# Joint attentions: sample keys in two halves a unit, two tiles turned per step, softmax in place, values and outputs for two heads

## The chip, the cores and the metric

The kernel runs on one core of one Trainium2 chip. The time is device microseconds (us) of one execution, median of several runs. The profiled execution is a further one, so its sums are made against its own time. TensorE (PE) multiplies, VectorE (DVE) and ScalarE (ACT) work element by element, GpSimd (POOL) prepares constants, and SyncE (SP) issues every transfer of the stages spoken of here, one after the other.

## The reference, cut to what matters

One inference step of a two-layer encoder: layer 0 has window attention (A) and differential attention (B), layer 1 a forgetting attention (C). Each mixer is applied to a prompt of 1024 frames and to eight running streams of 16 new frames each, whose keys and values of the past (2048 frames) lie in caches. A SwiGLU layer follows each mixer. What is computed in the part that changes:

```python
def _diff_attend(q, k, v, qpos, kpos, lam):        # B: 4 heads, 2 score maps each
    q2 = q.reshape(b, tq, B_HEADS, 2, HEAD_DIM)
    k2 = k.reshape(b, tk, B_HEADS, 2, HEAD_DIM)
    scores = jnp.einsum('bthed,bshed->bhets', q2, k2).astype(jnp.float32) * SCALE
    p = jax.nn.softmax(jnp.where(mask, scores, NEG_INF), axis=-1)
    attn = p[:, :, 0] - lam * p[:, :, 1]
    return jnp.einsum('bhts,bshd->bthd', attn.astype(v.dtype), v)

def _fox_attend(q, k, v, cq, ck, qpos, kpos):      # C: 16 heads
    scores = jnp.einsum('bthd,bshd->bhts', q, k).astype(jnp.float32) * SCALE
    scores = scores + jnp.moveaxis(cq, 1, 2)[..., :, None] - jnp.moveaxis(ck, 1, 2)[..., None, :]
    p = jax.nn.softmax(jnp.where(kpos[None, :] <= qpos[:, None], scores, NEG_INF), axis=-1)
    return jnp.einsum('bhts,bshd->bthd', p.astype(v.dtype), v)
```

All arrays are float32. HEAD_DIM is 64.

## The kernel before, in words

The program runs stages one after the other, each with its own buffers and semaphores: projection (`abp`), window attentions (`pa`, `sa`), the joint attention `jb` of B, merge and feed-forward (`abm`, `f0`), projection `c`, the joint attention `jc` of C, and again merge and feed-forward. The change is in `joint_attention`, which builds `jb` and `jc`, and in one place of `project_c`.

A joint attention does two things side by side. The **prompt** part has one head per unit (8 units in jb, 16 in jc) and eight tiles of 128 queries per head, in the order 3, 4, 2, 5, 1, 6, 0, 7; a tile t has t + 1 tiles of keys. One tile is one step s of the unit. The **sample** part has one unit per stream and group of eight score maps: 16 tiles of 128 past keys plus the new frames. The sample work of unit u is spread over the steps of the loop's pass u and of pass u + 1.

No engine is ordered by a scheduler: each engine's program is written out by hand and done strictly in that order. In pass u, at step s, with n = 8u + s:

- PE: `score(n+3)` (prompt scores), `turn(n+1)` (the exponentials transposed into PSUM), at s = 5 `score_new`, at s = 2 and 3 `turn_probs` (the sample's exponentials transposed, five groups), at s = 6 `turn_output`, then `attend(n)` (times the values, into `pv`), at s = 4 `attend_sample(u-1)`, and at s = 6 and 7 one `score_group` each, which multiplies the keys of two of the four partition groups of 32, all 16 tiles at once, in 32x32 pieces with 512 columns.
- DVE: at s = 0 `blocks` (queries laid out), `maximum(n+3)`, copies of some transposed groups, two or three `turn_keys` (`kt` from `kc`, a 32x32 block transpose, 3, 3, 3, 3, 2, 2, 0, 0 tiles at the eight steps), at s = 0 `maximum_sample(u-1)` (L1739), at s = 2 `inverse_sample`, and `output(n)` (L1712 or L1709), which frees `pv`.
- ACT: `exponential(n+2)`, copies of transposed groups out of PSUM (L1593), at s = 0 and 7 `copy_scores`, at s = 1 `exponential_sample`.

Transposed tiles go through `turned`, a ring of two PSUM slots. Which engine empties a slot is fixed by a table: every fourth prompt group by DVE, all others by ACT. PE may write a slot only when the group two places earlier has been copied out. `attend(n)` waits for `output(n-1)`, since `pv` has one buffer.

SP loads queries and keys of a head (`load_qk`), its values (`load_v`, once per head), the sample's keys in four parts, bias, new keys, values in four parts, and stores the head's output. Here are the places where the waits stand that matter below:

```python
            def score_group(u, first):
                if first == 0:
                    pe.wait_ge(kt_done, parts * per * (u + 1))
                    if u:
                        pe.wait_ge(scaled, u)
                pe.wait_ge(s_copied, 4 * u + first)
```

## Time and profile before

| | |
|---|---|
| median of 3 runs | 3878.53 us (3862.6 to 3883.28) |
| the profiled execution | 3852.3 us, its span 3850.6 us |
| busy in the span | PE 3470.9 us (90%), DVE 1623.8 us (42%), ACT 1068.1 us (28%), POOL 256.6 us (7%) |
| mean granted clock of TensorE | 0.943 |
| moved by transfers | 495.33 MB, 129 GB/s |
| stage jb | about 432 to 775 us of the span |
| stage jc | about 2147 to 2848 us of the span |

The profiled execution is 26 us shorter than the median of the three runs. In the rows of a profile the first numbers are start and duration (timeline) or sums (groups, waits); what stands in brackets is how long the engine sat idle before the instruction and what released it.

### The profile page before, as it was taken

The numbers are of one execution on the slowest core, as the hardware profiler recorded it, in microseconds if no ns is written. First come the engines' busy times: TensorE is split into PE (matmuls) and PEld (weight loads), VectorE is DVE, ScalarE is ACT, GpSimd is POOL, SyncE is SP. The second block draws the span as 40 slices with busy tenths as digits, with TensorE's granted clock in tenths as the row PEclk, the third lists the DMA queues.
The fourth block names the chain that finished last, engine by engine and source line by source line (L and its number), as shares of the span: only waits on it lengthen the run. The fifth ranks groups of instructions, "written<-read, shape, count | busy, mean of one in ns | idle before, by whom it ended". The sixth has DMA issues, their size and how long they took to land. (4 is left out here: it accounts for less than half of the span.)

```text
span 3850.6 us, 63167 instructions
## 1 busy us (share of the span) xinstructions
PE 3470.9 (90%) x25160; PEld 3003.2 (78%) x25160; DVE 1623.8 (42%) x2919; ACT 1068.1 (28%) x2130; POOL 256.6 (7%) x338
## 2 busy tenths in 40 slices
PE   8988588877999999996999689989979899999997
PEld 7866366666999999995899566666657799999997
DVE  5317466544334233336211265565543333333334
ACT  4215244333121111113221143344333211111211
POOL 2310000023000000004000000000003100000003
PEclk9999599988999999998999789999989899999999
DMA  5447598634111111103553888988842211111102
GB/s 171 120 138 162 143 284 271 222 140 131 44 33 35 52 44 33 54 22 124 144 173 105 213 242 255 276 257 256 276 156 104 77 54 44 33 54 37 40 22 104
DMA packets 421232, 495.33 MB, mean 129 GB/s; under 512 B 97968, under 2 KB 273616, under 8 KB 420880
## 3 DMA queue, kind: packets, MB, share of 16 engines
q1 hardware_dynamic: 421024, 492.45, 42.5%
q8 instruction: 143, 2.34, 0.3%
q14 instruction: 65, 0.53, 0.0%
HBM read 409.20 MB, written 84.10 MB: 128 GB/s over the span
## 5 line engine op out<-in xcount | busy, mean ns | idle before, releaser
L2426 DVE TENSOR_TENSOR f_gated<-f_gated,f_up 128x384 f32<-128x384 f32 x132 | 73.2, 555 | 741.2 <-ACT f_gated L2359 741.2
L2525 PE MATMUL f_gate<-m_ht_hi,f_w_hi 128*128 128x384 f32 x1056 | 355.3, 336 | 25.8 <-DVE f_w_lo L2418 25.8
L2450 DVE TENSOR_TENSOR f_y<-f_y,f_down 128x512 f32<-128x512 f32 x396 | 269.7, 687 | 229.4 <-PE f_down L2538 229.3
L2525 PE MATMUL f_gate<-m_ht_hi,f_w_lo 128*128 128x384 f32 x1056 | 354.9, 336 | 0.0
L2525 PE MATMUL f_gate<-m_ht_lo,f_w_hi 128*128 128x384 f32 x1056 | 354.8, 336 | 0.0
L2525 PE MATMUL f_up<-m_ht_hi,f_w_lo 128*128 128x384 f32 x1056 | 352.7, 334 | 0.0
L2525 PE MATMUL f_up<-m_ht_lo,f_w_hi 128*128 128x384 f32 x1056 | 352.7, 334 | 0.0
L2525 PE MATMUL f_up<-m_ht_hi,f_w_hi 128*128 128x384 f32 x1056 | 352.7, 334 | 0.0
L2538 PE MATMUL f_down<-f_wo_hi,f_act_hi 128*128 128x512 f32 x792 | 312.7, 395 | 10.6 <-DVE f_y L2450 9.3
L2538 PE MATMUL f_down<-f_wo_hi,f_act_lo 128*128 128x512 f32 x792 | 309.2, 390 | 0.0
L2538 PE MATMUL f_down<-f_wo_lo,f_act_hi 128*128 128x512 f32 x792 | 309.1, 390 | 0.0
L2359 ACT ACTIVATE f_gated<-f_gate 128x384 f32<-128x384 f32 x132 | 65.1, 493 | 684.5 <-PE f_up L2525 684.3
L2525 PEld LDWEIGHTS f_gate<-m_ht_hi,f_w_hi 128*128 128x128 f32 x1056 | 199.8, 189 | 27.4 <-issue 26.6
L1487 PE MATMUL jc_pv<-jc_vp,jc_probs_t 128*128 128x64 f32 x1152 | 157.5, 285 | 48.6 <-DVE jc_out L1712 47.8
L2525 PEld LDWEIGHTS f_gate<-m_ht_lo,f_w_hi 128*128 128x128 f32 x1056 | 199.8, 189 | 0.8
L2525 PEld LDWEIGHTS f_gate<-m_ht_hi,f_w_lo 128*128 128x128 f32 x1056 | 199.6, 189 | 0.0
L2525 PEld LDWEIGHTS f_up<-m_ht_hi,f_w_hi 128*128 128x128 f32 x1056 | 198.2, 188 | 0.0
L2525 PEld LDWEIGHTS f_up<-m_ht_lo,f_w_hi 128*128 128x128 f32 x1056 | 198.2, 188 | 0.0
L2525 PEld LDWEIGHTS f_up<-m_ht_hi,f_w_lo 128*128 128x128 f32 x1056 | 198.2, 188 | 0.0
L1487 PEld LDWEIGHTS jc_pv<-jc_vp,jc_probs_t 128*128 128x128 f32 x1152 | 149.4, 204 | 53.4 <-issue 50.4
L2538 PEld LDWEIGHTS f_down<-f_wo_hi,f_act_hi 128*128 128x128 f32 x792 | 149.1, 188 | 52.5 <-DVE f_y L2450 19.0
L2538 PEld LDWEIGHTS f_down<-f_wo_hi,f_act_lo 128*128 128x128 f32 x792 | 148.9, 188 | 31.7
(378 smaller groups left out, 6817.3 us busy)
## 6 DMA issues: line engine op xcount, KB each, us to landing
jc_kc<-in_cache_c_k SPq DMA_DIRECT2D x64, 1024.0 KB, 5.9
jc_vc<-in_cache_c_v SPq DMA_DIRECT2D x64, 1024.0 KB, 11.5
f_raw<-in_w_ffn_in SPq DMA_DIRECT2D x88, 512.0 KB
jb_kc<-in_cache_b_k SPq DMA_DIRECT2D x32, 1024.0 KB, 8.5
jb_vc<-in_cache_b_v SPq DMA_DIRECT2D x32, 1024.0 KB, 11.1
f_raw_o<-in_w_ffn_out SPq DMA_DIRECT2D x22, 1024.0 KB, 6.1
f_raw<-x SPq DMA_DIRECT2D x18, 512.0 KB, 4.1
abp_raw<-in_w_ab_in SPq DMA_DIRECT2D x32, 256.0 KB, 3.0
```

What stands on the lines that cost most here:

```text
L1487: last = pe.matmul(pv[:, 0:dv], probs_t[:, n % 2, x, :], vp[:, h % 2, x, :], start=(x == 0), stop=(x == t))
L2359: act.activation(silu[:, b], gate[:, q, 0:gw], ACT.Silu).then_inc(silu_done, 1)
L2426: dve.tensor_tensor(prod[:, b], silu[:, b], up[:, q, 0:gw], ALU.mult).then_inc(prod_done, 1)
L2450: dve.tensor_tensor(part, part, down[:, half, :], ALU.add).then_inc(added, 1)
L2525: last = pe.matmul(acc[:, q, 0:gw], a[:, s, k, u, :], b[:, k, token], start=(k == 0 and j == 0), stop=(k == KT - 1 and j == 2))
L2538: last = pe.matmul(down[:, half, :], a[:, s, t * P:(t + 1) * P], b[:, s, half * 512:(half + 1) * 512], start=(n == 0), stop=(n == 5))
```

## The change

- **Sample scores in halves.** `score_group` (two partition groups, 16 tiles, 512 columns) becomes `score_half(u, x, pair)`: half x of the tiles (8 tiles, 256 columns), partition groups in pairs. Half 0 of unit u is multiplied at step 4 of pass u, around `attend`, half 1 at step 0 of pass u + 1, around `attend`. ACT copies half 0 at step 5 and half 1 at step 1.
- **Keys turned** two tiles at each of the eight steps; `blocks` at step 2, `turn_new` at step 3.
- **The softmax of the samples** one step later: `maximum_sample` at the end of step 1 (after `output`), `exponential_sample` at step 2, in place (`s_probs` is `s_scores`), `inverse_sample` at 3, `turn_probs` at 3 (two groups) and 4 (three), `attend_sample` at 6, `scale_output` and `turn_output` at 7.
- **Who copies**: DVE copies both groups of step 3's tile and the second of step 5's; ACT all others.
- **Buffers**: `probs` has two buffers instead of three.
- **Values and outputs** of the prompt are loaded and stored for two heads at once, in jc in rows of 128 instead of 64 numbers. Loads are issued in another order; the last part of the keys comes behind the sample's values.
- **Start of a stage**: PE no longer waits for the last constants (`later`, `select`) before its first score but at step 4 of unit 0; the constants it needs first are set first.
- **Bias**: `project_c` writes `neg_c` sorted by partition group, so that jc loads rows of 512 numbers instead of 16 pieces of 32.

```diff
-                    dve.tensor_scalar(sum_s[:], sum_s[:], -1.0, None, ALU.mult).then_inc(sample_done, 1)
+                    dve.tensor_scalar(logf_s[:, 0:PAST].rearrange("p (a t r) -> p a t r", a=4, r=32),
+                                      sum_s[:, 0:PAST].rearrange("p (t a r) -> p a t r", a=4, r=32), -1.0, None,
+                                      ALU.mult).then_inc(sample_done, 1)
+                    dve.tensor_scalar(logf_s[:, PAST:], sum_s[:, PAST:], -1.0, None, ALU.mult).then_inc(sample_done, 1)
...
-    turns_at = ((0, 1, 2), (3, 4, 5), (6, 7, 8), (9, 10, 11), (12, 13), (14, 15), (), ())
-    probs_at = ((), (), (0, 1, 2), (3, 4), (), (), (), ())
+    half = parts * per // 2
+    probs_at = ((), (), (), (0, 1), (2, 3, 4), (), (), ())
+    dve_groups = ((3, 0), (3, 1), (5, 1))
...
-                use(("p", n, g), "dve" if (done + g) % 4 == 3 else "act")
+                use(("p", n, g), "dve" if (n % S, g) in dve_groups else "act")
...
-        vp = st.sb("vp", [P, 2, TILES_P, dv])
-        probs, probs_t = st.sb("probs", [P, 3, PROMPT]), st.sb("probs_t", [P, 2, TILES_P, P])
-        out = st.sb("out", [P, 2, TILES_P, dv])
+        vp = st.sb("vp", [P, 2, TILES_P, P])
+        probs, probs_t = st.sb("probs", [P, 2, PROMPT]), st.sb("probs_t", [P, 2, TILES_P, P])
+        out = st.sb("out", [P, 2, TILES_P, P])
...
+        s_scores = st.sb("s_scores", [P, keys])
+        s_probs = s_scores
...
+            def load_v(p):
+                if p >= 2:
+                    sp.wait_ge(pv_done, 2 * S * (p - 1))
+                c = v_cols(2 * p)
+                sp.dma_start(vp[:, p % 2], v[0:PROMPT, c:c + P].rearrange("(t p) d -> p t d", p=P)).then_inc(
+                    v_loaded[p % 2], 16)
...
+            load_keys(0, 0)
             load_q(0)
-            load_keys(0, 0)
             if diff:
                 sp.dma_start(lam[:], rows(b_lambda.rearrange("(a n) d -> a (n d)", a=1))).then_inc(lam_loaded, 16)
                 sp.dma_start(odd[:], row_odd).then_inc(lam_loaded, 16)
-            else:
+            load_keys(0, 1)
+            load_qk(1)
+            sp.wait_ge(setup, 12)
+            if not diff:
                 sp.dma_start(later[:], row_mask).then_inc(later_loaded, 16)
-                sp.wait_ge(setup, 12)
                 for a in range(4):
                     sp.dma_start(select[Q * a:Q * a + 8], selector[0:8]).then_inc(later_loaded, 16)
-                load_bias(0)
-            load_keys(0, 1)
-            load_qk(1)
-            load_v(1)
+            load_bias(0)
+            load_new_keys(0)
             load_keys(0, 2)
             load_keys(0, 3)
-            sp.wait_ge(setup, 12)
-            load_new_keys(0)
+            load_v(1)
...
-                    for x in range(parts):
-                        load_keys(u + 1, x)
+                    load_keys(u + 1, 0)
+                    load_keys(u + 1, 1)
+                if u + 2 < U:
+                    load_qk(u + 2)
+                if u + 1 < U:
+                    load_keys(u + 1, 2)
                     load_new_keys(u + 1)
                 load_values(u)
-                if u + 2 < U:
-                    load_qk(u + 2)
-                    load_v(u + 2)
-                store(u)
+                if u + 1 < U:
+                    load_keys(u + 1, 3)
+                if u % 2 == 1:
+                    if u + 3 < U:
+                        load_v((u + 3) // 2)
+                    store(u // 2)
...
-            def score_group(u, first):
-                if first == 0:
-                    pe.wait_ge(kt_done, parts * per * (u + 1))
-                    if u:
+            def score_half(u, x, pair):
+                if pair == 0:
+                    pe.wait_ge(kt_done, 2 * half * u + half * (x + 1))
+                    pe.wait_ge(q_done, 2 * (u + 1))
+                    if not diff:
+                        pe.wait_ge(bias_loaded[u % 2], 80 * (u // 2 + 1))
+                    if u and x:
                         pe.wait_ge(scaled, u)
-                pe.wait_ge(s_copied, 4 * u + first)
+                    pe.wait_ge(s_copied, 4 * u + 2 * x)
+                else:
+                    pe.wait_ge(s_done, 4 * u + 2 * x + 1)
...
+                                moving = bias[rows_a, u % 2, half * Q * x:half * Q * (x + 1)].rearrange(
+                                    "p (t r) -> p t r", r=Q)
+                            dst = s_ps[Q * c:Q * c + Q, a % 2, half * Q * pair:half * Q * (pair + 1)]
+                            last = pe.matmul(dst.rearrange("p (t r) -> p t r", r=Q), weights, moving,
...
-            pe.wait_ge(setup, 12)
-            if not diff:
-                pe.wait_ge(later_loaded, 80)
+            pe.wait_ge(setup, 8)
...
+                    if 1 <= u <= U and s == 0:
+                        score_half(u - 1, 1, 0)
+                    if u < U and s == 4:
+                        if u == 0:
+                            pe.wait_ge(setup, 12)
+                            if not diff:
+                                pe.wait_ge(later_loaded, 80)
+                        score_half(u, 0, 0)
                     attend(n)
-                    if 1 <= u <= U and s == 4:
+                    if 1 <= u <= U and s == 0:
+                        score_half(u - 1, 1, 1)
+                    if u < U and s == 4:
+                        score_half(u, 0, 1)
+                    if 1 <= u <= U and s == 6:
                         attend_sample(u - 1)
-                    if u < U and s >= 6:
-                        score_group(u, 2 * (s - 6))
-            for half in range(2):
-                slot = ring_slot(("fin", half))
+                    if 1 <= u <= U and s == 7:
+                        turn_output(u - 1)
...
+            def copy_scores(u, x):
+                act.wait_ge(s_done, 4 * u + 2 * x + 2)
                 if u:
-                    act.wait_ge(s_exp_done, u)
-                act.activation(s_scores[:, 0:PAST].rearrange("p (t a r) -> p a t r", a=4, r=Q)[:, a],
-                               s_ps[:, a % 2].rearrange("p (t r) -> p t r", r=Q), ACT.Copy).then_inc(s_copied, 1)
+                    act.wait_ge(turn_done, seq[("pt", u - 1, len(PG) - 1)] + 1)
+                dst = s_scores[:, half * P * x:half * P * (x + 1)].rearrange("p (t g b r) -> p b g t r", g=2, b=2, r=Q)
+                for b in range(2):
+                    act.activation(dst[:, b], s_ps[:, b].rearrange("p (g t r) -> p g t r", g=2, r=Q),
+                                   ACT.Copy).then_inc(s_copied, 1)
...
+                    if u >= 1 and s == 1:
+                        copy_scores(u - 1, 1)
+                    if u >= 1 and s == 2:
+                        exponential_sample(u - 1)
...
-                    if u < U and s == 0:
-                        blocks(u)
                     maximum(n + 3)
-                    if 1 <= u <= U and s == 5:
+                    if 1 <= u <= U and s == 7:
                         scale_output(u - 1)
                     copy_prompt(dve, "dve", n + 1)
                     if u < U:
-                        for t in turns_at[s][0:2]:
+                        for t in (2 * s, 2 * s + 1):
                             turn_keys(u, t)
-                        if s == 4:
+                        if s == 2:
+                            if u == 0:
+                                dve.wait_ge(setup, 12)
+                            blocks(u)
+                        if s == 3:
                             turn_new(u)
-                    if 1 <= u <= U:
-                        if s == 0:
-                            maximum_sample(u - 1)
-                        if s == 2:
-                            inverse_sample(u - 1)
-                        if s == 6:
-                            copy_out(u - 1)
+                    if 1 <= u <= U and s == 3:
+                        inverse_sample(u - 1)
                     output(n)
-                    if u < U:
-                        for t in turns_at[s][2:]:
-                            turn_keys(u, t)
+                    if 1 <= u <= U and s == 1:
+                        maximum_sample(u - 1)
+                    if 1 <= u <= U and s == 7:
+                        copy_out(u - 1)
```

On DVE, around the sample's maximum in a unit of jc, before:

```order
L1720 COPY jc_q_blocks<-jc_q_all 128x4x2x16 x2
L1686 TENSOR_REDUCE jc_neg_top<-jc_scores_b 128x1
L1728 STREAM_TRANSPOSE jc_kt<-jc_kc 128x512 x2
L1739 TENSOR_REDUCE jc_s_neg<-jc_s_scores 128x1
L1695 RECIPROCAL jc_inv<-jc_total 128x1
L1712 TENSOR_SCALAR jc_out<-jc_pv,jc_inv 128x64
L1728 STREAM_TRANSPOSE jc_kt<-jc_kc 128x512
L1686 TENSOR_REDUCE jc_neg_top<-jc_scores_a 128x1
L1595 COPY jc_probs_t<-jc_turned 128x384
L1728 STREAM_TRANSPOSE jc_kt<-jc_kc 128x512 x2
```

and with the change, the same place (`L1704` is `maximum`, `L1615` a copy out of `turned`, `L1746` `turn_keys`, `L1738` `blocks`):

```order
L1704 TENSOR_REDUCE jc_neg_top<-jc_scores_a 128x1
L1746 STREAM_TRANSPOSE jc_kt<-jc_kc 128x512 x2
L1714 RECIPROCAL jc_inv<-jc_total 128x1
L1730 TENSOR_SCALAR jc_out<-jc_pv,jc_inv 128x64
L1757 TENSOR_REDUCE jc_s_neg<-jc_s_scores 128x1
L1704 TENSOR_REDUCE jc_neg_top<-jc_scores_b 128x1
L1615 COPY jc_probs_t<-jc_turned 128x512
L1615 COPY jc_probs_t<-jc_turned 128x256
L1746 STREAM_TRANSPOSE jc_kt<-jc_kc 128x512 x2
L1738 COPY jc_q_blocks<-jc_q_all 128x4x2x16 x2
L1714 RECIPROCAL jc_inv<-jc_total 128x1
L1730 TENSOR_SCALAR jc_out<-jc_pv,jc_inv 128x64
```

The sample's maximum moved from ahead of the output of step 0 to behind the output of step 1; the two copies of step 3's tile now stand behind it and behind the prompt's maximum of step 2.

On PE, from the tile after the one whose output was waited for, before:

```order
L1465 MATMUL jc_scores_b<-jc_mask,jc_ident_b 128x128
L1474 MATMUL jc_turned<-jc_ident,jc_probs 128x128 x6
L1537 MATMUL jc_turned<-jc_ident,jc_s_probs 128x128 x12
L1487 MATMUL jc_pv<-jc_vp,jc_probs_t 128x64 x3
L1463 MATMUL jc_scores_a<-jc_k_both,jc_q_hi 128x128
L1464 MATMUL jc_scores_a<-jc_k_hi,jc_q_lo 128x128
L1465 MATMUL jc_scores_a<-jc_mask,jc_ident_b 128x128
L1474 MATMUL jc_turned<-jc_ident,jc_probs 128x128 x2
L1537 MATMUL jc_turned<-jc_ident,jc_s_probs 128x128 x4
L1537 MATMUL jc_turned<-jc_ident,jc_s_probs 16x128
L1487 MATMUL jc_pv<-jc_vp,jc_probs_t 128x64 x6
```

and with the change:

```order
L1468 MATMUL jc_scores_b<-jc_mask,jc_ident_b 128x128
L1477 MATMUL jc_turned<-jc_ident,jc_probs 128x128 x6
L1491 MATMUL jc_pv<-jc_vp,jc_probs_t 128x64 x3
L1466 MATMUL jc_scores_a<-jc_k_both,jc_q_hi 128x128
L1467 MATMUL jc_scores_a<-jc_k_hi,jc_q_lo 128x128
L1468 MATMUL jc_scores_a<-jc_mask,jc_ident_b 128x128
L1477 MATMUL jc_turned<-jc_ident,jc_probs 128x128 x2
L1549 MATMUL jc_turned<-jc_ident,jc_s_scores 128x128 x8
L1491 MATMUL jc_pv<-jc_vp,jc_probs_t 128x64 x6
```

The first eight transposes of the sample's exponentials stand one step later, behind the two of `turn(4)`; the remaining ones, and the first half of the next unit's scores, come at the step after.

## Rows read from the trace of the kernel before

**Rows 1.** Busy by stretch (jc, jb, one jc unit): stretch, length, PE, PEld, DVE, ACT, POOL, clock, DMA share, GB/s

```profile
2240.00:2760.00 520.00, 465.32 (x6200) 340.26 (x6200) 300.32 (x641) 206.56 (x463) 0.00 (x0) 0.93 0.88 263
495.00:730.00 235.00, 203.76 (x2714) 153.08 (x2715) 150.16 (x328) 96.20 (x219) 0.00 (x0) 0.95 0.90 277
...
2496.00:2537.00 41.00, 36.32 (x520) 26.36 (x509) 23.95 (x51) 16.33 (x37) 0.00 (x0) 0.96 0.88 265
```

**Rows 2.** Waits of PE in those stretches of jc and jb: us, times, longest us

```profile
PE jc_pv L1487 <- DVE jc_out L1712: 39.9, 13, 3.1
...
PE jb_pv L1487 <- DVE jb_out L1709: 10.1, 3, 3.4
```

**Rows 3.** Timeline of a jc unit at step 0 and 1: start, us, engine, what, [idle before]

```profile
2507.99 2.30 DVE L1739 TENSOR_REDUCE jc_s_neg<-jc_s_scores 128x1 f32<-128x2064 f32 x1
...
2510.82 1.55 PE L1487 MATMUL jc_pv<-jc_vp,jc_probs_t 128*128 128x64 f32 x10 [3.07 <-DVE jc_out L1712]
```

**Rows 4.** The sample's maximum by line: one per unit, first and last start; then one start

```profile
L1739 DVE TENSOR_REDUCE jc_s_neg<-jc_s_scores x16: 2302/2302/2304, 2215.9 to 2830.9; 128x1 f32<-128x2064 f32 x16
L1739 DVE TENSOR_REDUCE jb_s_neg<-jb_s_scores x8: 2302/2302/2303, 494.6 to 767.1; 128x1 f32<-128x2064 f32 x8
...
2548.57 2.30 DVE L1739 TENSOR_REDUCE jc_s_neg<-jc_s_scores 128x1 f32<-128x2064 f32 x1
```

**Rows 5.** Groups by line and shape in jc: busy us, mean ns of one, idle before

```profile
L1728 DVE STREAM_TRANSPOSE jc_kt<-jc_kc 128x512 f32<-128x512 f32 x256 | 168.7, 688 | 1.8 <-DMA jc_kc<-in_cache_c_k 1.6 <-issue 0.2
...
L1651 ACT ACTIVATE jc_s_probs<-jc_s_scores,jc_s_neg 128x2064 f32<-128x2064 f32 x16 | 32.3, 2016 | 24.8 <-DVE jc_s_neg L1739 24.8
...
L1595 DVE COPY jc_probs_t<-jc_turned 128x512 f32<-128x512 f32 x32 | 22.0, 686 | 3.3 <-PE jc_turned L1474 1.5
...
L1686 DVE TENSOR_REDUCE jc_neg_top<-jc_scores_b 128x1 f32<-128x896 f32 x16 | 17.0, 1060 | 1.9 <-PE jc_scores_b L1465 1.9
...
L1631 ACT ACTIVATE jc_probs<-jc_scores_b,jc_neg_top 128x896 f32<-128x896 f32 x16 | 16.0, 1002 | 0.8 <-DVE jc_neg_top L1686 0.8
```

**Rows 6.** Timeline of PE in jc's unit 0, which has no sample work yet

```profile
2177.75 0.36 PE L1463 MATMUL jc_scores_a<-jc_k_both,jc_q_hi 128*128 128x256 f32 x1
...
2182.48 0.39 PE L1474 MATMUL jc_turned<-jc_ident,jc_probs 128*128 128x128 f32 x2
2184.66 1.52 PE L1487 MATMUL jc_pv<-jc_vp,jc_probs_t 128*128 128x64 f32 x12 [1.79 <-DVE jc_out L1712]
```

**Rows 7.** The same unit, later: a wait of PE, and the granted clock around it

```profile
2191.06 0.45 PE L1474 MATMUL jc_turned<-jc_ident,jc_probs 128*128 128x128 f32 x1 [1.09 <-DVE jc_probs_t L1595]
...
2191.00:2191.50 0.50, 0.44 (x1) 0.18 (x1) 0.50 (x2) 0.50 (x2) 0.00 (x0) 0.50 1.05 365
```

**Rows 8.** Timeline of PE in a jc unit: a score group, what follows it, and attend_sample

```profile
2500.16 3.67 PE L1506 MATMUL jc_s_ps<-jc_kt,jc_q_blocks 32*32 32x512 f32 x64
...
2503.62 1.07 PE L1506 MATMUL jc_s_ps<-jc_bias,jc_select 32*32 32x512 f32 x16
...
2504.61 0.50 PE L1463 MATMUL jc_scores_b<-jc_k_both,jc_q_hi 128*128 128x512 f32 x1
...
2523.63 3.70 PE L1551 MATMUL jc_s_ps<-jc_vc,jc_s_probs_t 128*32 128x128 f32 x128
```

**Rows 9.** Timeline of both stages' starts, jc then jb

```profile
2147.62 0.47 SPq L1291 DMA_DIRECT2D jc_k_both<-hi_c  x1
...
2169.46 0.76 PE L1463 MATMUL jc_scores_a<-jc_k_both,jc_q_hi 128*128 128x512 f32 x1 [27.51 <-DMA jc_select<-in_head_rows]
...
2186.13 0.71 DVE L1728 STREAM_TRANSPOSE jc_kt<-jc_kc 128x512 f32<-128x512 f32 x1 [1.62 <-DMA jc_kc<-in_cache_c_k]
...
432.50 0.47 SPq L1291 DMA_DIRECT2D jb_k_both<-hi_ab  x1
...
441.98 0.77 PE L1463 MATMUL jb_scores_a<-jb_k_both,jb_q_hi 128*128 128x512 f32 x1 [13.23 <-DMA jb_q_lo<-lo_ab]
...
453.81 0.23 DVE L1774 CUSTOM_DVE_ANT_0 jb_lam<-jb_lam 128x64 f32<-128x64 f32 x1 [24.33 <-DMA jb_odd<-in_odd_heads]
```

More of the change, by code:

```diff
@@ L1473, in turn @@
                     for x in range(a, b):
-                        last = pe.transpose(slot[:, (x - a) * P:(x - a + 1) * P], probs[:, n % 3, x * P:(x + 1) * P], ident[:])
+                        last = pe.transpose(slot[:, (x - a) * P:(x - a + 1) * P], probs[:, n % 2, x * P:(x + 1) * P], ident[:])
                     last.then_inc(turn_done, 1)
@@ L1702, in output @@
                 dve.wait_ge(pv_done, n + 1)
-                if n % S == 0 and h >= 2:
-                    if not diff:
-                        dve.wait_ge(stored[h % 2], 16 * (h // 2))
-                    elif second:
-                        dve.wait_ge(stored[1], 16 * (h // 2))
+                if diff and n % S == 0 and h >= 2 and second:
+                    dve.wait_ge(stored[1], 16 * (h // 2))
+                if not diff and n % (2 * S) == 0 and h >= 4:
+                    dve.wait_ge(stored[h // 2 % 2], 16 * (h // 4))
                 if second:
```

116 lines of the change are left out of this document (46 added, 70 removed).

## Prediction

> **What bounds the kernel now.** Read the busy shares first: PE 90% of the span, DVE 42%, ACT 28%, so the question in the two joint attentions is what PE waits for. The stretches by time come next [rows 1]. In a steady stretch of jc PE is busy 465.32 of 520 us and its clock is 0.93 on average; in jb 203.76 of 235 us, clock 0.95. The transfers are at 0.88 and 0.90 of their engines, close behind. The length of a unit comes from the sample's maximum, done once a unit [rows 4]: (2830.9 - 2215.9) / 15 = 41.0 us in jc, (767.1 - 494.6) / 7 = 38.9 us in jb. So PE idles 54.7 / 520 x 41.0 = 4.3 us of a jc unit and 31.2 / 235 x 38.9 = 5.2 us of a jb unit.
>
> The waits of PE name most of it [rows 2]: once a unit `attend` of step 1 waits for `output` of step 0, 39.9 / 13 = 3.07 us in jc, up to 3.4 us in jb. The timeline shows why [rows 3]: DVE starts the sample's maximum at 2507.99 and is at it for 2.30 us. The output of step 0 stands behind it on DVE, and PE resumes at 2510.82. The rest, about 1.2 us in jc and 1.9 in jb, is PE and ACT taking turns at the two slots of `turned`. So the end is set by PE, and by DVE once a unit. The first thing to ask of the change is which DVE instruction PE will be waiting for when the maximum stands elsewhere.
>
> **1. The maximum behind step 1's output.** The stall of 3.07 us goes: output(0) no longer has it ahead. I then follow one jc unit from the moment when PE begins step 1 (time 0, both halves of the scores done), with full clock.
> PE: score(4), turn(2), attend(1), score(5), turn(3), attend(2), score(6). In unit 0 of before, free of sample work, the same row of instructions ran from 2177.75 to 2182.48 [rows 6]: 4.7 us. Then comes turn(4), which needs the ring slot that turn(3)'s first group held, and that group is now copied by DVE.
> DVE: prompt maximum to about 0.9, two key turns of 0.69 [rows 5] to 2.2, reciprocal and output(1) to about 2.65. ACT's two copies of the scores end by then too. The sample's maximum, 2.30 us, lasts to 4.95. Then the prompt maximum of 896 columns, 1.06, to 6.0, and the copy of 512 columns, 0.69, to 6.7 [rows 5]. PE stands from about 4.9 to 6.7: **1.8 us**.
> ACT: the exponential waits for the maximum and takes 2.02, to 7.1, then the prompt's exponential of 896 columns, 1.0, and only then turn(4)'s copy, to 8.6. The first of the two sample groups goes to PE at 7.1, the second needs that slot: PE stands 0.2 and then **0.95 us**. DVE's output(2), behind two more key turns and `blocks`, is done at 9.0, just in time.
> At step 4 PE and ACT alternate over three sample groups: about 0.5 us.
> Sum: 1.8 + 0.2 + 0.95 + 0.5 = 3.4 us of idle for 4.3 today. The stall moves by two steps and splits; only 0.9 us of it is gained in jc. In jb, by the same path with a slightly longer output, 3.6 for 5.2: 1.6 us.
>
> **2. Halves instead of groups.** Same columns in all, twice the number of multiplications. Today a group of 80 records (64 + 16) runs from 2500.16 to the next stage of PE at 2504.61 [rows 8]: 4.45 us. The 80 records are ten rounds of eight pieces side by side, so a round is about 0.43 us, and some 0.15 us is left for the change of tile shape. Four halves a unit cost four such borders instead of two: +0.3 us. A round of 256 columns should be half of 0.43, if its eight weight loads still hide. The nearest row is `attend_sample`: 128 pairs of load and multiplication in 3.70 us, 28.9 ns a pair [rows 8]; eight pairs at that pace are 0.231 us a round, against 0.215. With 40 rounds in a jc unit that is between 0 and 0.64 us; I take 0.2. Together +0.5 us a unit in jc, +0.4 in jb (32 rounds). It can't be below nothing, since no column is saved.
> The border itself is the place where a page speaks against this change: today's rows show the next stage's multiplication starting within some 0.15 us of the ten rounds' end [rows 8]. The Trainium skill, TensorEngine Tiling (Array Packing), Tiling Modes, says that a change of tiling mode drains TensorE. Row and rule agree that each border costs, and the row gives the price used.
>
> **3. The clock.** PE's clock has two levels, 1.2 and 2.4 GHz. Today each stall is followed by a stretch at the lower one. Units differ in how long it lasts: the unit from 2507.99 to 2548.57 is 40.6 us long at a mean clock of 0.96 [rows 1, 3, 4], against 41.0 on average at 0.93. So 0.03 of clock costs about 0.4 us, and the whole 0.07 about 1; half of the slow time, 0.07 x 41 = 2.9 us, bounds it from above. Will a stall split in two still bring the clock down? In jc's unit 0 the longest waits were 1.79 us at 2184.66 [rows 6] and 1.09 us before 2191.06, and by 2191 the clock was at 0.50 [rows 7]. The new pattern, 1.8 and 0.95 us within 3.7, is denser than that. I count nothing for the clock.
>
> **4. Turning, softmax in place, two buffers for `probs`.** Key turns are the same 16 at 0.69 us; at two a step they lie beside PE work, and DVE has room (23.95 us of 41 [rows 1]). Exponential n needs turn(n-2) of PE, which PE has done one step earlier: 0. The copies of new scores need the last sample transposes of step 4 and come at step 5: 0. `blocks` today waits for the score groups; that wait goes, but PE did not wait for it: 0. If the cover on DVE were gone, each turn would cost its 0.69.
>
> **5. Transfers.** In jb values are loaded once for two heads, in jc in longer rows, and the bias in 32 pieces instead of 512 a unit. SP's order is another: values behind the third part of the keys, the fourth part behind the values. Every load still has about a unit's time until it is used. PE and DVE wait for none in steady state today: all 256 key turns of jc waited 1.6 us for transfers [rows 5]. So 0. It would count only if units fell near 0.88 x 41 = 36 us. `project_c`'s sorted copy lies under PE-bound work: 0.
>
> **6. Starts.** jc: PE's first score waits until 2169.46 for the constants `select` [rows 9], queued behind a megabyte each of queries and keys. With the change it needs only the first head's queries and keys. In jb these were there 441.98 - 432.50 = 9.5 us after the first issue [rows 9]; in jc that gives 2147.62 + 9.5 = 2157.1, so 12.3 us earlier. But the key parts of unit 0 come through the same queue at the same pace, and DVE already waited 1.62 us for one at 2186.13 [rows 9]. I keep 9 us, bounds 0 and 12.3. jb: DVE waits for `lam` until 453.81 [rows 9], behind the same bytes in either order: 0.
>
> **Sum.** jc 15 x (0.9 - 0.5) = 6, jb 7 x (1.6 - 0.4) = 8, start 9: 23, say 25 us. The profiled execution's span of 3850.6 would become about 3826. The median of the runs, 3878.5, lies 26 us above the profiled execution's 3852.3; taken off it, 25 gives **3853 us**.
>
> **Rivals.**
> A. *The clock stays up.* Against it stand rows 6 and 7; for it, that the waits are each shorter than today's 3.07. It frees 1.0 to 2.9 us a unit; with 2, 22 x 2 = 44 more: 3809 us. The Trainium skill, TensorE: Matmul & The Clock Gate, Why this matters for your kernels, counts one long idle gap, about as long as today's, as what brings the clock down; by that rule this rival holds, since the new gaps are shorter. The fall near 2191 after no such gap speaks against the rule here.
> B. *The stall is shorter than I make it*, because DVE comes to the maximum earlier than 2.65 or the copies overlap. If both waits shrink to today's small ones of 1.2 us, 2.2 us a unit more and the clock with it: 22 x (2.2 + 2) = 92 more: about 3760 us.
> C. *Slower: the weight loads of the halves don't hide.* The place is the rounds of eight 32x32 pieces; there are 16 x 40 + 8 x 32 = 896 of them. For it: the same eight loads and eight multiplications a round have to be issued in half the time. Against it: `attend_sample` keeps 28.9 ns a pair. Each 0.01 us on a round costs 9 us. The 25 us hold 4 of that already, so the gain is gone from 0.215 + 29 / 896 = 0.247 us a round. At 0.27 it is 49 - 29 = 20 us slower: 3899 us.
> D. *The stall is only moved.* DVE's copy is later by one more key turn or ACT's copies are late, so the 0.9 and 1.6 go, and the halves' cost stays; with the start's 9 about nothing: 3875 us.
>
> **Chances.** The forecast 0.45, A 0.18, B 0.07, C 0.12, D 0.18. The likeliest one's own range, from the bounds of terms 1, 2 and 6, is 3835 to 3870. For 8 in 10 the range takes in A and D and part of C: 3800 to 3890. Faster by over 0.5% (19 us, about what a measurement of this kernel can tell from no change) takes A, B and three quarters of the forecast: 0.59. Within 0.5%: the rest of the forecast, most of D: 0.27. Slower: C and a little of D: 0.14.
>
> **What would show each step.** Right: the wait of `jc_pv` for `jc_out` is gone from PE's list; in its place `jc_turned` waits for DVE's copy `jc_probs_t`, about 1.8 us sixteen times, and a second wait behind ACT's `jc_probs_t` of about 1 us. The halves' rounds show 2.2 to 2.35 us a half. The first score of jc starts near 2157, jb's DVE start stays at 454. The distance between sample maxima is about 40.6 us in jc, 37.7 in jb. Wrong: the clock at 1.0 through steps 3 and 4 (A), no wait above 1 us (B), halves above 2.5 us (C), maxima as far apart as today (D).

## The result, and the profile after

| | before | after |
|---|---|---|
| median | 3870.63 us (3862.6 to 3883.28, 4 runs) | 3933.0 us (3928.38 to 3943.01, 4 runs) |
| profiled execution, span | 3852.3, 3850.6 us | 3928.38, 3926.6 us |
| PE busy | 3470.9 us, 25160 multiplications | 3566.8 us, 28744 multiplications |
| mean granted clock | 0.943 | 0.925 |

The ratio is 1.0162, with a 95% interval of 1.0121 to 1.0203: some 62 us slower, where 3853 us and a range of 3800 to 3890 were forecast. The ratios further down leave out one execution of e8 and one of e9 that ran over 1.5% longer than the fastest of their kernel (e9's, of 4044.63 us, is the one that was profiled, so its row has no columns from a trace).

From the page of the changed kernel (busy times; the granted clock in 40 equal slices, in tenths):

```profile
PE 3566.8 (91%) x28744; PEld 3132.9 (80%) x28744; DVE 1608.9 (41%) x2920; ACT 1069.6 (27%) x2130; POOL 258.1 (7%) x338
...
PEclk9999699888999999997999778887879899999999
```

The slices 23 to 30 (77888787) are the stage jc. The same stretches as in rows 1, of the changed kernel:

```profile
2240.00:2760.00 520.00, 474.44 (x7254) 381.01 (x7247) 257.46 (x563) 183.26 (x410) 0.00 (x0) 0.82 0.74 229
495.00:730.00 235.00, 204.83 (x3312) 164.36 (x3313) 141.18 (x316) 95.09 (x213) 0.00 (x0) 0.93 0.78 248
```

jc's clock fell from 0.93 to 0.82, jb's only from 0.95 to 0.93. PE is busier than before (474.44 for 465.32 us) and does less. The sample's maximum, once a unit, beside rows 4:

```profile
L1757 DVE TENSOR_REDUCE jc_s_neg<-jc_s_scores x16: 2291/2293/2303, 2217.0 to 2909.0; 128x1 f32<-128x2064 f32 x16
L1757 DVE TENSOR_REDUCE jb_s_neg<-jb_s_scores x8: 2291/2293/2302, 493.1 to 771.0; 128x1 f32<-128x2064 f32 x8
```

A unit of jc lasts (2909.0 - 2217.0) / 15 = 46.1 us instead of 41.0, one of jb 39.7 instead of 38.9: 77 us in jc, 5 in jb. PE's waits in 2240 to 2760 us of jc, beside rows 2:

```profile
PE jc_s_ps L1518 <- issue: 16.1, 10, 4.3
PE jc_turned L1477 <- DVE jc_probs_t L1615: 14.4, 7, 2.1
PE jc_turned L1549 <- ACT jc_probs_t L1613: 5.2, 11, 0.6
PE jc_turned L1536 <- issue: 2.5, 2, 1.5
PE jc_pv L1491 <- issue: 2.0, 2, 1.8
```

The old wait of `jc_pv` for `jc_out` is gone, and the wait for DVE's copy that the prediction names has come. The first row had not been foreseen: ten waits in the halves (L1518), put down to "issue", which means that the profile shows nothing PE waited for. The timeline of PE shows one:

```profile
2512.54 1.96 PE L1518 MATMUL jc_s_ps<-jc_kt,jc_q_blocks 32*32 32x256 f32 x64
2514.28 0.65 PE L1518 MATMUL jc_s_ps<-jc_bias,jc_select 32*32 32x256 f32 x16
2514.86 0.66 PE L1491 MATMUL jc_pv<-jc_vp,jc_probs_t 128*128 128x64 f32 x4
2515.45 1.50 PE L1518 MATMUL jc_s_ps<-jc_kt,jc_q_blocks 32*32 32x256 f32 x43
2519.14 1.49 PE L1518 MATMUL jc_s_ps<-jc_kt,jc_q_blocks 32*32 32x256 f32 x19 [2.18 <-issue]
```

PE stops for 2.18 us after 43 of 64 equal multiplications (a row counts what the profile recorded, two records for each multiplication of the program). The program has no wait between them; I read it so that the next instructions were not there yet. Then read the clock (the number before the DMA share):

```profile
2514.00:2516.00 2.00, 2.00 (x68) 1.29 (x55) 0.28 (x1) 0.10 (x2) 0.00 (x0) 1.00 1.04 382
2516.00:2518.00 2.00, 0.95 (x35) 0.33 (x19) 0.00 (x0) 0.00 (x0) 0.00 (x0) 1.00 1.05 383
2518.00:2520.00 2.00, 0.86 (x19) 0.45 (x27) 0.00 (x0) 0.00 (x0) 0.00 (x0) 0.51 1.13 251
2520.00:2522.00 2.00, 2.00 (x30) 0.73 (x14) 0.00 (x0) 0.00 (x0) 0.00 (x0) 0.50 1.00 193
...
2528.00:2530.00 2.00, 2.00 (x11) 1.90 (x10) 0.95 (x3) 0.00 (x0) 0.00 (x0) 0.50 0.92 333
2530.00:2532.00 2.00, 2.00 (x30) 1.83 (x32) 1.49 (x4) 1.71 (x3) 0.00 (x0) 0.57 0.08 26
```

It goes from 1.00 to 0.50 (from 2.4 to 1.2 GHz) during the stop, at about 2518, and stays there until about 2531.5, while PE is busy from 2519.14 on: 2 us of stop, then 12 us of work at half speed.

### The profile page after: what moved, and what is told of

Its sections match the earlier page's. It is cut to its first block and busy times, and to the rows that moved or that the text cites. A ratio compares the mean times of both kernels' runs of the same rounds, so it can differ in the third digit from the quotient of the medians.

```text
span 3926.6 us, 70338 instructions
## 1 busy us (share of the span) xinstructions
PE 3566.8 (91%) x28744; PEld 3132.9 (80%) x28744; DVE 1608.9 (41%) x2920; ACT 1069.6 (27%) x2130; POOL 258.1 (7%) x338
## 3 DMA queue, kind: packets, MB, share of 16 engines
q1 hardware_dynamic: 392544, 490.36, 40.6%
## 5 line engine op out<-in xcount | busy, mean ns | idle before, releaser
L1491 PEld LDWEIGHTS jc_pv<-jc_vp,jc_probs_t 128*128 128x128 f32 x1152 | 181.6, 241 | 17.3 <-issue 17.3
L1491 PE MATMUL jc_pv<-jc_vp,jc_probs_t 128*128 128x64 f32 x1152 | 188.8, 323 | 3.8 <-issue 2.0
L1613 ACT ACTIVATE jc_probs_t<-jc_turned 128x512 f32<-128x512 f32 (+2 forms) x144 | 68.1, 488 | 397.8 <-PE jc_turned L1477 397.5
```

The costliest lines, as they stand in the source:

```text
L1491: last = pe.matmul(pv[:, 0:dv], probs_t[:, n % 2, x, :], vp[:, h // 2 % 2, x, first:first + dv], start=(x == 0), stop=(x == t))
L1613: eng.activation(dst, src, ACT.Copy).then_inc(act_emptied, 1)
```

## The experiments

Theory I: PE's own instructions come too late once their number in the halves doubles, and the short stops bring the clock down. Theory II: the clock falls because of where the waits for copies now stand. Theory III: the order of the transfers does it.

For each kernel the table gives the ratio to the kernel before on the same chip, the length of a jc unit, PE's idle time in it and the part put down to issue. The last two columns come from the granted clock read in steps of half a microsecond from 2240 to 2780 us: how often it fell (a stretch at the lower level that already ran at 2240 is counted), and the share of time at the lower level. Each row is read from one execution; that of e7 was 29 us shorter than e7's median, that of e4 12 us. e12 is the kernel of e9. The kernel before, run beside the others, took 3849 to 3858 us.

| kernel | ratio (95%) | unit | idle | issue | falls | low |
|---|---|---|---|---|---|---|
| before | 1 | 41.0 | 4.3 | 0.05 | 13 | 15% |
| after | 1.0162 (1.0121 to 1.0203) | 46.1 | 4.3 | 2.3 | 20 | 34% |
| e1_wide | 0.9933 (0.9905 to 0.9960) | 41.1 | 3.3 | 0.3 | 13 | 18% |
| e2_split | 1.0484 (1.0449 to 1.0518) | 51.7 | 5.8 | 2.7 | 12 | 57% |
| e3_order | 1.0142 (1.0110 to 1.0174) | 44.8 | 3.8 | 1.4 | 19 | 32% |
| e4_maxlate | 0.9988 (0.9965 to 1.0012) | 40.7 | 4.0 | 0.4 | 9 | 13% |
| e5_less | 1.0094 (1.0071 to 1.0118) | 44.1 | 3.7 | 1.2 | 19 | 31% |
| e6_groups | 1.0210 (1.0183 to 1.0237) | 44.3 | 4.6 | 0.9 | 14 | 27% |
| e7_copyfirst | 1.0207 (1.0186 to 1.0228) | 43.8 | 5.1 | 0.9 | 14 | 24% |
| e8_pieces | 0.9891 (0.9848 to 0.9934) | 40.2 | 3.5 | 0.6 | 5 | 14% |
| e9_start | 0.9877 (0.9839 to 0.9914) | | | | | |
| e10_spread | 1.0150 (1.0111 to 1.0190) | 44.6 | 4.2 | 2.0 | 21 | 30% |
| e11_halfmax | 1.0151 (1.0113 to 1.0190) | 45.1 | 4.1 | 2.3 | 19 | 33% |
| e12_start2 | 0.9892 (0.9855 to 0.9928) | 39.8 | 3.5 | 0.5 | 4 | 13% |
| e13_both | 0.9823 (0.9786 to 0.9860) | 38.2 | 2.7 | 0.2 | 5 | 7% |

What stands around the falls, by the timeline of PE (a fall goes with a stop when it starts in it or up to 2.3 us behind it): before, all 13 go with the stall of 3.07 us. In the changed kernel 7 of the 20 go with the wait at turn(4) and 13 with an issue wait, of 0.5 to 4.3 us. In e1 all 13 go with the wait at turn(4). The quick rows don't bring the clock down by themselves: those from 2539 to 2545, without a stop, left it at 1.00, and it fell at 2552 with the wait at turn(4).

**Number of instructions.** e1, on the changed kernel:

```diff
-                for step in range(4 if diff else 5):
+                steps_here = (0, 2) if diff or pair else (0, 2, 4)
+                for step in steps_here:
...
-                                moving = kt[rows_a, half * x:half * x + half, Q * hb:Q * hb + Q]
+                                moving = kt[rows_a, half * x:half * x + half, Q * hb:Q * hb + 2 * Q]
...
-                            dst = s_ps[Q * c:Q * c + Q, a % 2, half * Q * pair:half * Q * (pair + 1)]
+                            dst = s_ps[Q * c:Q * c + Q, a % 2]
```

> The changed kernel, in which each half multiplies 512 columns at a time with half as many loads and multiplications (of the four products of a half two are left out, and the bias is multiplied with the first pair alone; both stages). Columns, order and waits stay. Theory I (PE's own instructions come too late once their number doubles, and the short stops bring the clock down): the waits put down to issue in jc (some 25 us between 2150 and 2920) fall to 3 us or less, a jc unit goes from 46.8 to 41 to 42 us, the time to 3845 to 3865 us. Theory II (the clock falls because of where the waits for copies now stand): the unit stays at 46 to 47 us, the time at 3925 to 3940. Theory III (the transfers' order sets it): as II.

Measured: 3835.22 us for 3857.24 before, some 10 us below what theory I expected; a unit is 41.1 us. The issue waits are gone from the halves, the waits for the copy are all there; windows and waits of e1 in 2240 to 2760:

```profile
2240.00:2760.00 520.00, 480.25 (x6169) 345.94 (x6169) 296.19 (x643) 207.83 (x469) 0.00 (x0) 0.90 0.82 259
...
PE jc_turned L1477 <- DVE jc_probs_t L1615: 26.8, 13, 2.2
...
PE jc_s_ps L1563 <- issue: 1.3, 1, 1.3
```

Theory I holds, II and III fall as the main cause: the same waits for copies, the same order of transfers, and the clock is back at 0.90. From 1.0162 to 0.9933 is 0.023 of 3870: **89 us** (60 to 115 by the ends of the two intervals) hang on the number of instructions. With the columns kept, half as many are also twice as long; the two can't be told apart here.

e2, on the kernel before. Two sums now alternate in one bank, and part of the products of past keys is lost in them; the work stays:

```diff
-                for step in range(4 if diff else 5):
+                for step, x in [(step, x) for step in range(4 if diff else 5) for x in range(2)]:
+                    cols, some = slice(256 * x, 256 * x + 256), slice(8 * x, 8 * x + 8)
...
-                                weights, moving = q_blocks[rows_a, hb // 2, hb % 2], kt[rows_a, :, Q * hb:Q * hb + Q]
+                                weights, moving = q_blocks[rows_a, hb // 2, hb % 2], kt[rows_a, some, Q * hb:Q * hb + Q]
```

> The kernel before, in which each multiplication of 512 columns in score_group is issued as two of 256, in the same place and order otherwise. Theory I (number of instructions): issue waits appear on PE in jc and the unit goes from 41.2 to 45 to 47 us, jb a little longer, the time to 3930 to 3960 us. Theories II (place of the waits) and III (order of transfers): nothing but the 0.016 us a round that my step 2 allowed, 3865 to 3885 us.

Measured: 4047.73 us, 190 us more than before: the direction of theory I, twice the size that it expected and three times the changed kernel's loss. Windows of e2, then its PE in the first group of a unit, 160 pairs of load and multiplication in a row:

```profile
2240.00:2760.00 520.00, 464.02 (x6407) 358.97 (x6414) 232.77 (x498) 159.43 (x360) 0.00 (x0) 0.72 0.71 207
...
2474.46 3.24 PE L1507 MATMUL jc_s_ps<-jc_kt,jc_q_blocks 32*32 32x256 f32 x109
2480.06 1.49 PE L1507 MATMUL jc_s_ps<-jc_kt,jc_q_blocks 32*32 32x256 f32 x18 [2.36 <-issue]
```

The rounds themselves are as fast as my step 2 made them (29.7 ns a pair); after 109 pairs in 3.24 us PE stands 2.36 us. The clock then stays low for 26 us on average, so that it has less time to fall again (12 falls, 57%).

**Transfers.** e3, on the changed kernel:

```diff
-                    load_keys(u + 1, 0)
-                    load_keys(u + 1, 1)
-                if u + 2 < U:
-                    load_qk(u + 2)
-                if u + 1 < U:
-                    load_keys(u + 1, 2)
-                    load_new_keys(u + 1)
+                    for x in range(parts):
+                        load_keys(u + 1, x)
+                    load_new_keys(u + 1)
                 load_values(u)
-                if u + 1 < U:
-                    load_keys(u + 1, 3)
+                if u + 2 < U:
+                    load_qk(u + 2)
```

> The changed kernel with the loop's transfers issued in the order of before (all four parts of the keys and the new keys, then the values, then queries and keys of the head after next); values and outputs still move for two heads. Theory III (the last part of the keys behind the values makes transfers come in bursts, and PE's instructions, which come through the same engines, are late in them): the share of time with no transfer falls, issue waits fall to under 8 us, the unit to 41 to 43 us, the time to 3850 to 3880 us. Theory I without the order: 3925 to 3940 us. Theory II: 3925 to 3940 us.

Measured: 3917.66 us; the interval overlaps that of the changed kernel. Issue waits went from 2.3 to 1.4 us a unit (21 us in the stage, not under the 8 of theory III), the falls hardly. The order is no main cause.

e5, on the changed kernel:

```diff
+                n = span if u == 0 else P
-                sp.dma_start(kc[:, x], k_cache[stream_of(u), x * span:(x + 1) * span, columns_of(u)].rearrange(
+                sp.dma_start(kc[:, x, 0:n // P], k_cache[stream_of(u), x * span:x * span + n, columns_of(u)].rearrange(
```

and the same for `vc`.

> The changed kernel with all its instructions, in which from a stage's second unit on only one of every four tiles of the sample's cached keys and values is transferred (three quarters of them are left out; both stages). Supply through the transfer engines (PE's instructions come late because they share the engines with keys and values): issue waits in jc fall from some 36 us to 5 or less, the clock there returns to 0.91 or more, the unit to 41 to 42 us, the time to 3840 to 3865 us. Rival (twice the number of pairs is too much for PE whatever is transferred, or the clock falls for the shorter multiplications themselves): the unit stays at 45 us or more, the time at 3910 to 3940 us.

Measured: 3889.37 us, between the two. Windows and the first issue wait of e5:

```profile
2240.00:2760.00 520.00, 475.26 (x7484) 381.25 (x7484) 274.16 (x599) 192.06 (x429) 0.00 (x0) 0.85 0.38 101
...
PE jc_s_ps L1520 <- issue: 13.7, 6, 4.3
```

With the transfers at 0.38 for 0.74, issue time goes from 2.3 to 1.2 us a unit and no further, and falls from 20 to 19. Traffic makes the instructions later (1.0162 and 1.0094 are some 26 us apart); but they are late with half of it too.

**Place.** e10, on the changed kernel:

```diff
                     if u < U and s == 5:
+                        score_half(u, 0, 1)
                         score_new(u)
...
+                    if 1 <= u <= U and s == 1:
+                        score_half(u - 1, 1, 1)
...
                     attend(n)
-                    if 1 <= u <= U and s == 0:
-                        score_half(u - 1, 1, 1)
-                    if u < U and s == 4:
-                        score_half(u, 0, 1)
```

> The changed kernel with the second pair of each half moved away from the first: to step 5 and to step 1, ahead of attend, so that no more than 40 or 61 of the quick pairs of load and multiplication stand in a row where it was 80 and more with a short attend between. The number is the same. If PE's instructions fall behind only in long quick rows: issue waits in jc fall from 36 us to 15 or less, falls of the clock from 20 to about 14 in 540 us, the time to 3885 to 3910 us. If it is the number in a unit that counts, wherever they stand: 3925 to 3940 us.

Measured: 3910.75 us, a ratio of 1.0150. By the microseconds it touches the first expectation, but the ratio is that of the changed kernel, and the mechanism of the first one failed: issue 2.0 us a unit, 21 falls. Moving the second row of each half by one step does not help.

**Undoing the halves.** e6: `score_group` of before at steps 6 and 7 and its `turns_at`, in the changed kernel.

```diff
-                        score_half(u, 0, 0)
                     attend(n)
...
-                    if 1 <= u <= U and s == 6:
+                    if 1 <= u <= U and s == 5:
                         attend_sample(u - 1)
+                    if u < U and s >= 6:
+                        score_group(u, 2 * (s - 6))
```

> The changed kernel with the halves alone undone: groups of 512 columns over all 16 tiles at steps 6 and 7 and keys turned 3, 3, 3, 3, 2, 2 as before; the softmax stays a step later and in place, attend_sample stands at step 5. Theory I (number of instructions) and the e1 result of 3835 us: 3825 to 3850 us, units of 41 us, no issue wait over 1 us in score_group. If the place of the halves and not their number had made the stops, 3900 us or more. My steps 1 and 6 without step 2 give 3857 - 13 - 12 - 9 = 3823 us.

Measured: 3932.43 us, a clear miss, and not a clean undoing. Windows and waits of e6:

```profile
2240.00:2760.00 520.00, 466.41 (x5749) 342.52 (x5756) 270.41 (x593) 191.57 (x430) 0.00 (x0) 0.86 0.76 238
...
PE jc_turned L1477 <- DVE jc_probs_t L1601: 31.1, 12, 3.1
PE jc_s_ps L1555 <- issue: 6.8, 3, 2.6
```

With three tiles turned at steps 0 and 1 the sample's maximum starts some 0.4 us later against PE, a third key turn (0.70 us) stands between it and the prompt's maximum, and the wait at turn(4) grows from 2.05 to 3.06 us. And `attend_sample`, at step 5 between `score_new` and the groups, now meets issue waits itself (6.8 us). So the doubled instructions are not the only way to such a loss: with 512 columns a unit is 44.3 us here. Of its 14 falls 10 go with the wait at turn(4) and last 9 us on average, for 6.1 with the stall of the same length in the kernel before; 3 go with issue waits. Why the same stop costs more at this place is not shown.

e7, on e6: at step 2 DVE's `copy_prompt` ahead of `maximum(n + 3)`.

```diff
+                    if s == 2:
+                        copy_prompt(dve, "dve", n + 1)
                     maximum(n + 3)
```

> As e6, and at step 2 DVE copies the transposed tile of step 3 ahead of the prompt's maximum of 896 columns instead of behind it. By step 1 of the prediction PE's stall at turn(4) is 1.8 us, of which this maximum is 1.06: it should fall to 0.8 to 1.1 us, the unit by about 1 us, and the time by 15 to 25 us against e6. Rival (what PE no longer waits for there it waits for behind ACT at the sample's groups, as in e4): within 5 us of e6.

Measured: 3933.73 us. The wait went from 3.06 to 2.09 us as worked out, and the time is that of e6: the rival's outcome.

**The maximum.** e4, on the kernel before:

```diff
-                        if s == 0:
-                            maximum_sample(u - 1)
...
                     output(n)
+                    if 1 <= u <= U and s == 0:
+                        maximum_sample(u - 1)
```

> The kernel before with one edit: the sample's maximum stands behind output of step 0 instead of ahead of it. My step 1 says that the 3.07 us stall goes; the exponential of the samples then starts about 1 us later and has room until step 2. If that holds, 2 to 3 us a jc unit are gained and the time is 3820 to 3845 us. Rival (the stall only moves to the next copy behind ACT, or the clock falls in another place): 3865 to 3880 us.

Measured: 3855.56 us for 3857.24: the rival's mechanism, 10 us below its range. One wait of 3.07 became three; waits of e4, 2240 to 2760:

```profile
PE jc_turned L1537 <- ACT jc_probs_t L1593: 20.6, 21, 1.3
PE jc_turned L1474 <- DVE jc_probs_t L1595: 10.7, 13, 0.8
PE jc_pv L1487 <- DVE jc_out L1712: 8.1, 13, 0.6
```

e8, on e4: the maximum in pieces.

```diff
+            def maximum_first(u):
+                dve.wait_ge(s_copied, 4 * u + 2)
...
+                dve.tensor_reduce(s_part[:, 0:1], by_tile[:, :, 0:2 * Q], AX.XY, ALU.max, negate=True).then_inc(part_done, 1)
...
+                    if u < U and s == 7:
+                        maximum_first(u)
```

> The kernel before, with the sample's maximum in two pieces of about 1.15 us: over the first two partition groups behind output of step 7, over the others behind output of step 0 (and two small reductions to join them). With whole maximum behind step 0's output (e4) PE stood 0.6, 0.8 and 1.3 us in turn and the clock fell 9 times in 540 us of jc, the time was 3856. Theory (short waits of PE below 1 us leave the clock up): the wait of 1.3 us shrinks to about 0.3, falls of the clock to 5 or fewer in the same stretch, a jc unit to 39 us or less, the time to 3815 to 3840 us. Rival (the pieces cost DVE more than they free, the stall returns at step 7's output): 3850 to 3875 us.

Measured: 3829.08 us, faster than before by 0.7 to 1.5%. Windows and waits of e8:

```profile
2240.00:2760.00 520.00, 475.03 (x6330) 343.50 (x6315) 309.79 (x694) 208.08 (x473) 0.00 (x0) 0.93 0.89 263
495.00:730.00 235.00, 204.61 (x2770) 150.84 (x2768) 159.98 (x367) 104.01 (x238) 0.00 (x0) 0.99 0.90 276
...
PE jc_turned L1538 <- ACT jc_probs_t L1594: 21.5, 25, 1.3
PE jc_s_ps L1552 <- issue: 8.9, 5, 2.7
```

The waits behind ACT are still up to 1.3 us, against my expectation; but they bring the clock down once in 540 us. The other four of the five falls follow the issue waits of L1552 (`attend_sample`) within 4 us; one of them lasts 44 us. In jb the clock is 0.99.

e9 and e12 are one kernel: e8 with the change's start, sorted bias, values and outputs for two heads and the softmax in place (their lines are those of the change's diff).

> As e8, with those parts of the change that add no instruction to PE: the start of a stage, the sorted bias, values and outputs for two heads, the softmax in place. My step 6 says 9 us less than e8, of which the trace of the changed kernel leaves 8 at the first score; steps 4 and 5 say 0 for the rest. Rival (the first units wait for the keys and the gain at the start is lost by the first sample's maximum): as e8 within 3 us.

> The kernel of e9 once more, for an undisturbed profile of the best version. 3805 to 3825 us; in jc no wait of PE above 1.4 us in a steady unit except issue waits in attend_sample, five falls of the clock or fewer in 540 us, first score of jc near 2161, a unit of 39 to 40 us.

Measured: 3815.14 and 3808.15 us, ratios 0.9877 and 0.9892: about 1.1% faster than before, 2.7% faster than the changed kernel. In e12's trace the unit (39.8 us), the waits (up to 1.3 us outside `attend_sample`) and the falls (4) are as expected; the first score of jc is at 2138.3 and not near 2161, since the stages ahead of it got shorter too. Against e8 no difference in time can be told; the first maximum of jc comes at 2196.6 for e8's 2208.2.

**The two stops together.** e11, on the changed kernel (the maximum of the first half at step 6), and e13 (e11 with e1's edit):

```diff
+                    if u < U and s == 6:
+                        maximum_first(u)
```

> The changed kernel, in which the maximum of the first half's scores is taken at step 6 already and only that of the second half (1040 columns) behind step 1's output. PE's stall of 2.05 us at turn(4) should fall to about 0.9; its own late instructions (issue waits, some 36 us in jc) stay. If the stalls at turn(4) and the issue waits each bring the clock down by themselves, of the 20 falls in 540 us some 8 (behind turn(4)) go and 12 stay: unit 44 us, the time 3890 to 3910 us. If the issue waits alone matter: 3920 to 3935. If the stall at turn(4) alone matters: 3830 to 3850.

> The changed kernel with both: the maximum in halves (as e11) and 512 columns a multiplication with half the pairs (as e1; two of the four products of a half and the second pair's bias are left out). If the two kinds of stop are what the change cost, falls of the clock in 540 us of jc go to 5 or fewer, the unit to 38 to 39.5 us and the time to 3780 to 3815 us. If something else keeps the clock low (the short prompt stages around the halves), 3830 us as e1.

Measured: 3913.63 us (1.0151), in none of e11's three ranges, and 3787.83 us (0.9823), as e13's first outcome said (its fifth fall is behind a wait of 4.8 us at the end of the stage). Waits of e11, then windows and waits of e13:

```profile
PE jc_s_ps L1519 <- issue: 16.0, 10, 3.0
PE jc_turned L1478 <- DVE jc_probs_t L1616: 8.3, 7, 1.2
...
2240.00:2760.00 520.00, 485.99 (x6780) 345.10 (x6787) 315.90 (x713) 218.69 (x493) 0.00 (x0) 0.97 0.84 264
...
PE jc_turned L1478 <- DVE jc_probs_t L1616: 15.4, 13, 1.3
PE jc_turned L1550 <- ACT jc_probs_t L1614: 12.4, 24, 0.6
```

| ratio | wait at turn(4) 2.05 us | 1.2 us |
|---|---|---|
| doubled instructions | 1.0162 | 1.0151 |
| half of them | 0.9933 | 0.9823 |

The shorter wait alone gives nothing that can be told (20 falls and 19; six of e11's follow a wait of 1.2 us at turn(4) with one of 0.6 behind it). Without the late instructions it gives 0.011, some 43 us. e11's three outcomes had assumed that the causes add; they don't.

## Why the prediction was wrong, by its own steps

**Step 1, the stall: right in place and size, but its gain in jc did not come.** Foreseen were 1.8 us at turn(4) and 0.95 at the second sample group; measured 2.05 (2.4 in jb) and 0.60. Sixteen of the first were foreseen in jc; the changed kernel has ten, and where one is missing between 2240 and 2760 the clock was low already, so that PE came behind the copy. e1, where all of these waits stand, has a unit of 41.1 us for before's 41.0, with 40.6 foreseen: its idle time fell by 1.0 us, but the lower level lasts longer (18% of the time for 15%, 0.6 us a unit). In jb the gain came, 37.7 us as foreseen. Idle time was to be 3.4 us a unit and is 4.3, of which 2.3 are issue. Without the late instructions it is 3.3 (e1).

**Step 2, the halves: the sum right, and the step that failed.** It charged 0.5 us a unit for twice the number of multiplications; their late issue alone stops PE for 2.3 us a unit, in no term of the sum. A half takes 2514.86 - 2512.54 = 2.32 us at full clock, with 2.2 to 2.35 foreseen. What failed is the question it asked: whether the eight weight loads of a round hide. I answered it with `attend_sample`, 128 pairs at 28.9 ns [rows 8]. That one row of quick pairs keeps pace does not say that PE can be fed at this pace when a unit has four more such rows. Such a row can be late itself: in the kernel before once, by 0.74 us, in e8 five times, up to 2.7 us. Before, the pairs of the groups took 4.45 / 80 = 56 ns each, and with the halves 2.32 / 80 = 29.

**Step 3, the clock: 0 counted, nearly the whole loss.** This term stood at nothing, and the runs put 4.8 us a unit in its place. PE's idle time in a jc unit is 4.3 us before and after. The share at the lower level went from 15% of 41.0 to 34% of 46.1 us, 6.2 and 15.7 us. Half of the difference, 4.8 us a unit, is lost work: 15 x 4.8 = 71 of jc's 77 us. My bound, that half of today's slow time is the most that can be at stake, looked only at a gain. The clock was at stake in the other direction too.

**Steps 4 and 5: 0 held** for the softmax in place and the values for two heads (e12 against e8) and nearly for the order of the transfers (e3). Two buffers of `probs` were not tried alone.

**Step 6, the start: 12 us for 9.** The first issue of the stage jc and its first score, in the changed kernel:

```profile
2151.75 0.46 SPq L1295 DMA_DIRECT2D jc_k_both<-hi_c  x1
...
2161.56 0.76 PE L1466 MATMUL jc_scores_a<-jc_k_both,jc_q_hi 128*128 128x512 f32 x1 [15.35 <-DMA jc_k_hi<-ck]
```

2161.56 - 2151.75 = 9.8 us, where the prediction read 9.5 off jb; before it was 2169.46 - 2147.62 = 21.8 us. That is 12.0 us, close to the bound of 12.3. By the clock of the span the score is only 7.9 us earlier, since jc starts 4.1 us later. At the first maximum 3 of the 12 are left in the changed kernel (65.3 us behind the first issue for 68.3), in e1 11.6 (56.7). jb's 0 held, with 1.5 us.

**The sum.** With the late instructions out of the way, the rest of the change gives 22 us (e1: 3835.22 for 3857.24), where 25 were forecast. That they are so near is partly luck: jc's 6 us did not come (15 x 0.1 = 2 us the other way), the start gave 12 for 9, and jb about its 8.

**The rivals.** C had the right place and the wrong mechanism: the rounds did not grow, they are 2.32 / 10 = 0.232 us at full clock, border included, below its threshold of 0.247, and its 3899 us fell short by 34. A, that shorter waits keep the clock up, describes e8 (waits for other engines up to 1.3 us, 5 falls) and not the changed kernel, where all 15 stops of 1.17 to 2.2 us went with a fall. That is against the rule of the Trainium skill, TensorE: Matmul & The Clock Gate, Why this matters for your kernels, as the prediction used it (one long idle gap, about as long as today's 3.07 us): the trace does not bear it out as a safe bound. D, that the stall is only moved, describes e4's mechanism.

**Open** is why the lower level lasts 3, 7, 10, 14 or, rarely (in e2 mostly), 17 to 44 us after stops that look alike, and why some stops bring no fall: in e4 PE stood 2.10 and 1.64 us before `attend_sample` with the clock left at 1.00. Open too is why jb lost only 5 us with issue waits of 1.8 us a unit. What makes the instructions late is shown only as far as number and, in part, traffic; how far ahead they are held is not shown.

## What to carry to other kernels

Count the instructions of an engine per microsecond, not only their columns: where pieces are halved and each lasts 29 instead of 56 ns, the supply of instructions can run out between two of them, and the profile then says "issue" in the middle of equal instructions. Price a short stop of TensorE with what follows it: read the granted clock for some 15 us behind each stop before counting it at its own length. And cut a long operation of a helping engine (here the maximum, 2.3 us) into pieces before moving it; moved whole, it only chooses who waits.

## What the runs showed of the hardware

- A row of 64 equal multiplications of 32x256 was interrupted by 2.18 us with no wait in the program; another stopped for 2.36 us after 109 pairs in 3.24 us (e2). This remains, at about half, with the transfers at 0.38 instead of 0.74 (e5).
- In the changed kernel the clock fell with all 15 stops of 1.17 to 2.2 us, and with three of 0.5 to 1.0 us; it fell behind 4 of e13's 13 pairs of waits of 1.2 and 0.6 us, but in 540 us only once behind waits of 0.6 and 1.3 us that came every unit (e8), and not at all with issue waits of 2.10 and 1.64 us in e4.
- A single fall lasted 44 us in e8 and in e12 while PE was busy nearly all the time, and 3 to 17 us behind nearly all other stops of the kernels with 512 columns or with the change (once 38 us in e6, once 24 in e3).
